# Expert loop of a mixture-of-experts kernel: bias rows of an expert loaded to four partitions and spread by a vector shuffle, in place of selector products

## The reference, cut to what matters

```python
logits = (t @ w_router + b_router)
top_val, top_idx = lax.top_k(logits, TOP_K)           # TOP_K = 4 of N_EXPERTS = 32
probs = jax.nn.softmax(top_val, axis=-1)
...                                                   # rows sorted by expert
def expert_block(args):
    xb, e = args
    gu = xb @ w_gate_up[e] + b_gate_up[e]             # 1024 -> 2048
    x_glu = jnp.minimum(gu[:, 0::2], 7.0)
    x_lin = jnp.clip(gu[:, 1::2], -7.0, 7.0)
    act = x_glu * jax.nn.sigmoid(1.702 * x_glu) * (x_lin + 1)
    return act @ w_down[e] + b_down[e]                # 1024 -> 1024
...
out = jnp.einsum('tk,tkd->td', probs, y_pairs)
```

## Time and profile before

| | us |
|---|---|
| runs without a profile: lowest, median, highest | 3802.69, 3803.28, 3808.03 |
| the profiled execution as a whole | 3806.89 |
| its span from first to last instruction | 3805.1 |
| PE busy / DVE busy / ACT busy in the span | 3185.7 / 1077.3 / 647.6 |
| expert loop: first up products to the last rows added | 2553.6 to 3741.1 |
| weights loaded in it | 384 tiles of 1 MB |
| mean TensorE clock granted in the span | 0.903 of full |

### The profile page before, as it was taken

The page is one execution under the profiler, slowest core; times in us unless marked ns, Lnnn a source line. Parts: engine busy times, 40 slices in busy tenths (PEclk is TensorE's granted clock), DMA queues, the critical chain, the costliest instruction groups (busy, mean ns, idle before and its releaser), DMA issues.

```text
span 3805.1 us, 44308 instructions
## 1 busy us (share of the span) xinstructions
PE 3185.7 (84%) x18944; PEld 1617.3 (43%) x18944; DVE 1077.3 (28%) x2009; ACT 647.6 (17%) x1340; POOL 194.5 (5%) x180
## 2 busy tenths in 40 slices
PE   6896679999788888999999976728899989989873
PEld 3552234444333444566666654413344433333331
DVE  3341330000422121145555554331112111111114
ACT  0131100000001222234433442000111101101100
POOL 0000000000000000011111111020000000000001
PEclk9996789999897888999999996759999999999986
DMA  3114212212100000411111100065777899999993
GB/s 144 45 56 174 103 44 78 76 56 88 47 31 18 18 28 28 160 39 44 51 39 39 39 34 2 9 222 234 311 305 314 360 404 379 386 395 385 398 375 149
DMA packets 119322, 581.11 MB, mean 153 GB/s; under 512 B 12806, under 2 KB 24086, under 8 KB 72534
## 3 DMA queue, kind: packets, MB, share of 16 engines
q1 hardware_dynamic: 92274, 531.69, 35.6%
q10 hardware_dynamic: 20436, 24.26, 1.8%
q0 software_dynamic: 6416, 22.32, 1.6%
HBM read 549.76 MB, written 28.47 MB: 152 GB/s over the span
## 4 chain that ended last, share of the span: by engine, by line
PE 73%; DMA 12%; DVE 9%; ACT 3%; issue 2%; POOL 1%; SPq 0%; DVEq 0%; POOLq 0%; ACTq 0%
PE product_banks L768 35%; PE product_banks L1011 12%; DMA space<-in_wgu 8%; PE product_banks L1033 7%; PE score_banks L814 4%; PE score_banks L942 3%; PE turn_bank L799 3%; PE out_bank L836 2%; DVE rstd L1340 1%; DMA space<-in_wt 1%; PE turn_bank L827 1%; PE product_banks L755 1%; DMA y_rows<-zeros 1%; PE turn_bank L1022 1%; DVE space L1544 1%
## 5 line engine op out<-in xcount | busy, mean ns | idle before, releaser
L768 PE MATMUL product_banks<-space 128*128 128x512 f32 (+3 forms) x4064 | 1453.5, 511 | 56.4 <-DVE space L1471 15.3
L768 PEld LDWEIGHTS product_banks<-space 128*128 128x128 f32 (+1 forms) x4064 | 711.5, 193 | 711.5 <-issue 621.3
L1011 PE MATMUL product_banks<-space 128*32 128x512 f32 x5440 | 630.0, 608 | 64.0 <-DMA space<-in_wgu 62.5
L1011 PEld LDWEIGHTS product_banks<-space 128*32 128x32 f32 x5440 | 180.0, 111 | 451.7 <-issue 327.9
L1033 PE MATMUL product_banks<-space,rstd 128*32 128x256 f32 x5440 | 332.3, 399 | 46.4 <-ACT rstd L1275 30.3
L1663 DVE TENSOR_TENSOR sq<-product_banks,space 128x512 f32<-128x512 f32 x85 | 58.8, 692 | 758.4 <-PE product_banks L1011 758.4
L1033 PEld LDWEIGHTS product_banks<-space,rstd 128*32 128x32 f32 x5440 | 207.0, 115 | 152.6 <-issue 83.5
L1118 ACT ACTIVATE space<-product_banks 128x512 f32<-128x512 f32 (+2 forms) x238 | 113.0, 526 | 881.9 <-PE product_banks L768 879.0
L814 PE MATMUL score_banks<-space 64*128 64x256 f32 (+5 forms) x352 | 173.6, 598 | 34.9 <-ACT space L1132 17.9
L799 PE MATMUL turn_bank<-sq,cst 128*128 128x512 f32 (+1 forms) x196 | 107.0, 685 | 112.3 <-DVE sq L1336 112.0
L684 POOL TENSOR_TENSOR space<-space 128x512 f32<-128x512 f32 x112 | 133.8, 1209 | 1180.0 <-ACT space L1214 1087.4
(11 more groups left out here) (241 smaller groups left out, 2154.6 us busy)
## 6 DMA issues: line engine op xcount, KB each, us to landing
space<-in_wgu SPq DMA_DIRECT2D x256, 1024.0 KB, 13.9
space<-in_wdn SPq DMA_DIRECT2D x128, 1024.0 KB, 20.7
space<-in_wt SPq DMA_DIRECT2D x104, 1024.0 KB, 5.4
y_rows<-zeros ACTq DMA_DIRECT2D x2, 6400.0 KB, 27.7
y_rows<-zeros ACTq DMA_DIRECT2D x85, 128.0 KB
space<-in_wt SPq DMA_DIRECT2D x12, 512.0 KB, 4.3
space<-in_wt SPq DMA_DIRECT2D x8, 576.0 KB, 3.8
x<-in_xT SPq DMA_DIRECT2D x1, 2048.0 KB, 15.8
```

Of the source, the lines that this page charges most:

```text
L768: ins = nc.tensor.matmul(bank[0:rows, at:at + cols], lhsT, rhs, start=(i == 0), stop=(i == len(mm) - 1))
L1011: ins = nc.tensor.matmul(bank[ROWS * g:ROWS * g + ROWS, :], xT_[:, k, :], w[:, 512 * g:512 * g + 512], start=(k == 0), stop=(k == DC - 1))
```

## The change

For each expert SP now issues two small DMAs behind its twelve tiles: the up bias as 4 rows of 2 KB and the down bias as 4 rows of 1 KB, to partitions 0, 32, 64 and 96 of a buffer of 128 x 768 (`raw_bias`, two of them). VectorE waits for them at the expert's first block and copies, with one shuffle in which all 32 partitions of a group read the group's partition 0, to `biasb`. The selector, the two products, the two copies on ScalarE and the load of all biases are gone, and so are the waits of TensorE for the bias. Two clears of the new buffers come before the loop, and SP waits for them once. In the extra block SP waits for the shuffle of position 30, issues that expert's bias ahead of its first tile, and VectorE makes the shuffle.

```diff
-        sig, sel = ms[:, 0:256], ms[:, 256:256 + P]
+        sig = ms[:, 0:256]
+        raw_bias = [bias_rows, arena[:, 768:1536]]
...
@@ sync
-                sp.dma_start(bias_rows[:, 0:512], bgu.rearrange("e (g n) -> (e g) n", g=4)).then_inc(s_brow, 16)
-                sp.dma_start(bias_rows[:, 512:768], bdn.rearrange("e (g n) -> (e g) n", g=4)).then_inc(s_brow, 16)
                 sp.wait_ge(s_tab, 1)
+                def load_bias(e, to, signal):
+                    heads = to[0:P:ROWS, :]
+                    sp.dma_start(heads[:, 0:512], bgu[bass.ds(e, 1), :].rearrange("a (g n) -> (a g) n", g=4)).then_inc(signal, 16)
+                    sp.dma_start(heads[:, 512:768], bdn[bass.ds(e, 1), :].rearrange("a (g n) -> (a g) n", g=4)).then_inc(signal, 16)
...
                         sp.dma_start(tile_slot(g, t), tile_source(e, t)).then_inc(s_w[g % NS], 16)
+                    if q == 0:
+                        sp.wait_ge(s_bzero, 1)
+                    elif q >= 2:
+                        sp.wait_ge(s_bc, q - 1)
+                    load_bias(e, raw_bias[q % 2], s_brow[q % 2])
...
                 with sp.Fori(0, n_more) as b:
                     e = sp.value_load(tab_i[0:1, bass.ds(b + 2 * N_EXP, 1)], min_val=0, max_val=N_EXP - 1)
+                    sp.wait_ge(s_bc, b + N_FIXED)
+                    load_bias(e, raw_bias[0], s_bmore)
@@ tensor
-            pe.wait_ge(s_brow, 32)
-            def expert_bias(n):
-                pe.wait_ge(s_picks, n + 1)
-                pe.wait_ge(s_bc, n)
-                nc.tensor.matmul(PO[:, :], sel, bias_rows[:, 0:512], start=True, stop=True)
-                nc.tensor.matmul(PT[:, 256:512], sel, bias_rows[:, 512:768], start=True, stop=True).then_inc(s_bp, 1)
...
             def fixed_down(j):
-                pe.wait_ge(s_bc, position_of[min(j + 1, N_FIXED_BLOCKS - 1)] + 1)
...
-                if first:
-                    expert_bias(q)
...
-                expert_bias(b + N_FIXED)
                 turn_inputs(b + N_TURNS)
...
-                pe.wait_ge(s_bc, b + N_FIXED + 1)
@@ scalar
-            def copy_bias(n, to):
-                act.wait_ge(s_bp, n + 1)
-                nc.scalar.activation(to[:, 0:512], PO[:, :], F.Copy)
-                nc.scalar.activation(to[:, 512:768], PT[:, 256:512], F.Copy).then_inc(s_bc, 1)
...
-                act.wait_ge(s_y, n)
-                copy_bias(b + N_FIXED, biasb[0])
                 copy_inputs(b + N_TURNS, xTb[0])
@@ vector
+            V.memset(raw_bias[0], 0.0)
+            V.memset(raw_bias[1], 0.0).then_inc(s_bzero, 1)
-            def pick(n, col):
-                V.tensor_scalar(sel, const("group_of"), col, None, ALU.is_equal).then_inc(s_picks, 1)
+            def spread_bias(source, to):
+                V.stream_shuffle(to, source, [0] * 32).then_inc(s_bc, 1)
...
                 if j == FIRST_AT[q]:
+                    dve.wait_ge(s_brow[q % 2], 32 * (q // 2 + 1))
+                    if q >= 2:
+                        dve.wait_ge(s_y, FIRST_AT[q - 1])
+                    spread_bias(raw_bias[q % 2], biasb[q % 2])
                     dve.wait_ge(s_bc, q + 1)
                 gated(j, UP[j % 2], biasb[q % 2], actb[j % 2])
-                if j == FIRST_AT[q] and q + 1 < N_FIXED:
-                    pick(q + 1, four_e[:, q + 1:q + 2])
...
                 n = b + N_FIXED_BLOCKS
-                dve.wait_ge(s_bp, b + N_FIXED)
-                pick(n, four_more[:, bass.ds(b, 1)])
+                dve.wait_ge(s_y, n)
+                dve.wait_ge(s_bmore, b * 32 + 32)
+                V.memset(small[:, 11:12], 0.0)
+                spread_bias(raw_bias[0], biasb[0])
                 dve.wait_ge(s_bc, b + N_FIXED + 1)
```

15 lines of the change are left out of this document (4 added, 11 removed).

## The result

The changed kernel ("after") took 3810.06 us (median of 20 runs; 3799.39 to 3815.67), the kernel before 3804.01 us in the 20 runs beside it (3797.55 to 3808.03). The ratio is 1.0016, 95% interval 1.0009 to 1.0023: 6 us slower (3 to 9), where 4 us faster was forecast. The time is inside the given range, but the kernel moved the other way. The profiled execution of after took 3809.57 us with a span of 3807.7, 2.6 more than before; the profiled execution of before lies 2.9 us above the median of its runs, so the two traces differ by less than the medians do.

A forecast was written before the change was run, and what follows sets the result against it. The prediction took the DMA queue as the bound, in the later half four engines that carry the stores. Its terms, -1.3 - 2.0 + 5.0 + 3.6 - 9.5 = -4.2 us, gave 3799.1 us, range 3789 to 3812.

The forecast's parts named there:

- first block (first to 2): At the very first block up(0) waits for no tiles, so without the bias products it starts earlier: gain 1.3 us.
- one-block positions: Behind one-block experts tiles are asked for late, so removing the products gains 1.5 us at position 4, 0.5 at position 2.
- late turns and transfers to position 10: Turns at positions 4 and 8 each 2.5 us late, 5.0 in all, plus the small transfers' cost up to position 10.
- transfers from 10 to 30: The share of the small bias transfers' 3.6 us that falls behind position 10, at 0.15 us an expert.
- extra block (30 to rows): At the end, up no longer waits behind VectorE: gated 11.8 us earlier, less 2.3, gain 9.5 us, between 5 and 12.
- The new wait: VectorE waits for bias behind tile 11; 3.6 us from landing to turn makes positions 4 and 8 each 2.5 us late.
- The transfers: 3 KB more an expert on the four store engines: 0.15 us at some 24 of 31 experts, 3.6 us in all.
- the share of a store that runs alone: The last store of expert rows shows share 0.26, read as four engines carrying the stores and bounding the later half.
- rival on the landing: Two rivals: bias lands early, 3789.7 us, chance 0.17; or spread comes 2 us later, 3811.6 us, chance 0.17.
- the products that go: 1.49 us of TensorE per expert removed: free at big positions, gaining 1.3 at the first block and 2.0 at one-block ones.
- SP's delay in the extra block: SP waits for position 30's spread and issues the extra tiles 3.8 us later, delaying the last store by 0.8 us.
- the first rival: Bias lands early, so no late turns, free transfers and SP punctual, extra block giving 10.3: 3789.7 us, chance 0.17.

The follow-up runs named there:

- experiments 1: Changed kernel with each expert's two bias loads issued ahead of its tile 5, not behind tile 11, from position 1 on: 3800.21 us, ratio 0.9986.
- experiment 4: Kernel before without selectors, bias products and copies at positions 2 to 30, which use the bias of position 0 or 1: 3807.98 us, ratio 1.0007.
- experiment 3: Kernel before with the two small bias loads added behind tile 11 of each position, into partitions nobody reads: 3809.90 us, ratio 1.0014.
- experiment 10: Changed kernel with four DMAs per store: late bias 3758.46 us; bias ahead of tile 5 3742.47; that with sigmoid before stores 3749.31, or with products put back 3743.99.
- Experiment 9: Kernel before with each 128 KB store of a block's rows issued as four DMAs of 32 KB, not one: 3751.18 us, ratio 0.9858.
- experiment 8: Changed kernel with the extra block's bias loads and SP's wait for position 30's spread moved behind that block's tile 6: 3806.30 us, ratio 1.0003.

## Why the prediction was wrong

The forecast's own terms against the table (after less before, one trace each):

| step | forecast | measured in the traces |
|---|---|---|
| first block (first to 2) | -1.3 | +1.5 |
| one-block positions (2 to 4; position 2's share stands in the line above) | -2.0 | -0.7 |
| late turns and transfers to position 10 (4 to 10) | +5.6 | +5.6 |
| transfers from 10 to 30 | +3.0 | +3.3 |
| extra block (30 to rows) | -9.5 | -7.0 |
| behind the rows | 0 | +2.7 (scatter) |
| sum | -4.2 | +5.4 |

(The forecast's 5.0 for the waits and 3.6 for the transfers are divided here at position 10, with 0.15 for each of the 20 positions behind it. Ahead of the loop after was 2.9 us early, which gives the 2.6 us between the spans, with rounding. The sum without the scatter line is +2.7, and the times say 3 to 9. That the third line agrees to a tenth is partly luck: single traces of kernels with an early bias lie between 242.3 and 247.2.)

**The new wait was right.** The shuffle, gated and the 2.5 us at positions 4 and 8 came as worked out (2.8 and 2.5 in the parts of 4 to 10); tile 11 by the forecast's own step of 11.4 us behind tile 7 would have landed at 2752.2, and the shuffle started at 2752.37. But at position 8 the lower clock makes the turn as late without it (14.9 and 15.4 us behind tile 7 in experiments 1 and 4), so half of this term has two causes, and to move the bias alone gives only the other half back.

**The transfers were right,** 0.15 us an expert forecast, 3.2 / 20 = 0.16 in experiment 3, and nothing in experiment 10, once the stores were spread. By the rule of the Trainium skill named in the prediction ("DMA: Bandwidth & Descriptors", section "Why a DMA increments its semaphore by 16 and not by 1") 32 rows divide over sixteen engines where four groups go over four. Experiment 9 agrees, by 54 us; the share of a store that runs alone, which the prediction also called, does not tell the two apart. Neither rival on the landing held: the wait was neither early nor 2 us late.

**The step that failed first is "the products that go".** The forecast treated 1.49 us of TensorE's time as a saving or as nothing, 3.3 us of gain in all, and had no term for the clock. It was work that TensorE did while it waited, and with it went part of its clock. The first block shows it bare. TensorE's timeline of before, from the first input transposes to the second:

```profile
2549.20 1.94 PE L1002 MATMUL score_banks<-cst,space 128*128 128x128 f32 x8 [66.49 <-DMA space<-h_rows,space]
2550.93 1.92 PE L995 MATMUL out_bank<-space,ms 128*128 128x512 f32 x2
2552.64 1.06 PE L996 MATMUL turn_bank<-space,ms 128*128 128x256 f32 x2
2553.63 7.12 PE L1011 MATMUL product_banks<-space 128*32 128x512 f32 x64
2560.69 1.09 PE L1002 MATMUL score_banks<-cst,space 128*128 128x128 f32 x8
```

And that of after:

```profile
2546.29 1.94 PE L1006 MATMUL score_banks<-cst,space 128*128 128x128 f32 x8 [65.99 <-issue]
2549.47 9.69 PE L1015 MATMUL product_banks<-space 128*32 128x512 f32 x64 [1.24 <-ACT space L1261]
2559.09 1.09 PE L1006 MATMUL score_banks<-cst,space 128*128 128x128 f32 x8
```

The up products start as soon as the copy of the inputs has ended, 3.2 us behind the first transposes where it was 4.4: the 1.3 us are there. Then they take 9.69 us, not 7.12. TensorE stood still for 1.24 us ahead of them, and it starts them at the lower clock. The stage of before that begins just ahead of its up products:

```profile
2553.00:2557.00 4.00, 4.00 (x34) 1.04 (x36) 0.00 (x0) 2.16 (x3) 0.00 (x0) 0.90 0.41 135
```

And that of after:

```profile
2549.00:2553.00 4.00, 3.53 (x20) 0.90 (x24) 0.00 (x0) 1.70 (x2) 0.47 (x1) 0.50 0.45 135
```

From transposes to transposes it is 12.8 us against 11.5: 1.3 lost in the place of 1.3 gained. That repeats. The 64 up products take 7.1 to 7.6 us in all five kernels that have the products in this gap, and 8.4 to 9.9 in all ten that do not; from transposes to transposes the five take 11.5 to 11.9 and the ten 11.5 to 13.0. So in none was the 1.3 us gained. In the loop the mean clock goes from 0.95 to 0.92, position 8 pays 2.4 to 2.9 us for it (experiments 1 and 4), and experiment 4 bounds what the removal is worth at 1 us of gain to 6 of loss. And at the one-block position 3 the issues do not come forward by what was booked: 2 to 4 takes 89.1 us after and 89.8 before, 89.5 in experiment 4, and 89.3 to 89.6 in three of the other kernels that have the products. The low clock at position 2 moves this stretch by 3 us, more than the products do.

**The second step that failed is SP's delay in the extra block.** The mechanism and the size of its cause were right (SP 3.8 us late by the forecast; 10.55 less the loop's 6.72 of delay is 3.8), but its effect was put at 0.8 us on the last store and 1.5 on TensorE. Measured: the last store lands 3728.90 - 3720.27 - 6.7 = 1.9 us late, and from gated to rows TensorE's side takes 9.7 us for 7.0, 2.7 more (its down products 6.12 us). With the order of experiment 8 the end gains 11.1, and with an early bias 10.9. So the first rival's price of a punctual SP (10.3) was near.

Had the products' step been 0 and SP's effect been known, the sum would have been +1 to +2. The rest up to 6 us stays unassigned: it is within what the times and one trace each can tell.

## What to carry to other kernels

Work taken off TensorE while it is waiting saved nothing here: look at the granted clock in the stretch behind it, and book small products in a gap at zero, not at their duration. A load in four rows cost time here as long as the stores were cut in four too; ask first whether the few engines of such DMAs are the bound, since undoing that was worth nine times the whole effect of this change. Where two causes end in the same delay, taking one away shows nothing: position 8 needed a kernel without each. And where a load's buffer is freed late, issue it where the free buffer is old news (ahead of the tiles, or behind the ones that are ready), not at the head of the queue.

## What the runs showed of the hardware

- A store of 128 KB cut in four groups holds back a queue of 1 MB loads so far that the same bytes as four DMAs of plain rows shorten the loop from position 10 to 30 by 36 us in 690; the sixteen engines then move 417 GB/s late in the loop, before 377.
- Two loads of 8 and 4 KB in four rows each cost 0.16 us together in a queue bound in this way (3.2 us in 20 positions), and four more 0.20 (3.9 in 20), though nobody uses their data. With the stores spread they cost nothing that shows (653.9 us without, 653.1 to 655.1 with them).
- One pair of products of 1.5 us per expert moved TensorE's mean granted clock in the loop: 0.95 with 1012.56 us busy in 1120, and 0.92 with 990.31 without the pair. Over the whole span no execution with it was under 0.902 and none without it over 0.899.
- A low clock (0.50) in the 4.4 us behind tile 7 of position 2 made the turn about 3 us late (14.8 to 15.7 us for 12.4), and 2 to 4 about 3 us longer; the same clock difference cost nothing from 10 to 30, where the DMA queue is the bound.
- After 66 us in which TensorE stood still, 64 products of 512 columns took 8.4 to 9.9 us with 1.24 us of idle time just ahead of them, and 7.1 to 7.6 with two small products in that gap.
- The spread of 128 x 768 by one shuffle takes 1.04 us, and its pattern 14 ns.
